# Second layer's normed rows and output rows turned between weight chunks, squares by block, linear attention's half products in turn, narrow products loaded wide

## The reference, cut

```
for l in range(2):                     # first block
    h  = rms(x,  norm_w[l]) * (1 + scale)   + shift      # 256 latent rows
    hc = rms(xc, norm_w[l]) * (1 + scale_c) + shift_c    # 256 context rows
    ... = project_stream(h, w_in[l], ...)                # 2048 -> 4160 + 2048 (z) columns
    x = x + gate * ((concat(o_a, o_b, o_c) * silu(z)) @ w_out[l])
    # xc likewise in layer 0 only

def gla_chunked(q, k, v, log_a):       # second block, 4 heads, chunks of 64 rows
    def step(state, xs):
        q_c, k_c, v_c, dec = xs
        o = einsum('bhcd,bhde->bhce', q_c, state)
        state = state * dec + einsum('bhcd,bhce->bhde', k_c, v_c)
        return state, o
```

## Time and profile before

| | |
|---|---|
| median of 3 runs | 3891.92 us |
| the profiled execution | 3893.01 us |
| its span | 3891.2 us |
| mean granted clock of TensorE | 0.972 |
| PE, busy share | 94% |
| DVE, ACT | 52%, 43% |
| HBM read | 148 GB/s |

### The profile page before, as it was taken

One profiled execution on the slowest core, in us unless ns is written; L12 is line 12 of the kernel. 1 busy time (PEld: TensorE's weight loads), 2 busy tenths in 40 slices (PEclk: granted clock), 3 DMA queues, 4 the chain that ended last, 5 costly groups with the idle time before them and its releaser, 6 DMA issues.

```text
span 3891.2 us, 46277 instructions
## 1 busy us (share of the span) xinstructions
PE 3647.3 (94%) x18672; PEld 2943.5 (76%) x18672; DVE 2013.7 (52%) x3118; ACT 1670.0 (43%) x2696; POOL 68.0 (2%) x118
## 2 busy tenths in 40 slices
PE   7899999999898799999899999999999799999998
PEld 2677777887776677778677777766777599999776
DVE  1666654344567646642355544435455466666444
ACT  2323344434421423455544434444445555455433
POOL 1200000000020000000000000000000000000000
PEclk8999999999999999999999999999999999999999
DMA  9643322233364455223355566635555356666554
GB/s 363 187 146 114 98 60 55 58 103 100 108 191 150 134 173 179 87 64 108 93 180 160 160 178 178 179 103 159 179 173 178 103 163 186 188 185 188 180 184 162
DMA packets 351045, 577.49 MB, mean 148 GB/s; under 512 B 25316, under 2 KB 131060, under 8 KB 348912
## 3 DMA queue, kind: packets, MB, share of 16 engines
q1 hardware_dynamic: 344512, 549.47, 45.7%
q0 software_dynamic: 6320, 25.06, 2.3%
HBM read 570.26 MB, written 4.19 MB: 148 GB/s over the span
## 4 chain that ended last, share of the span: by engine, by line
PE 56%; DVE 4%; ACT 3%; DMA 2%; issue 1%; DVEq 0%; SPq 0%; ACTq 0%
PE ps L703 36%; PE ps L1576 13%; DVE w_lo L672 1%; PE ps L1272 1%; DMA raw_ring<-in_w_in_dram 1%; ACT w_hi L666 1%; PE ps L1076 1%; PE ps L1184 1%; PE ps L1453 1%; PE ps L1460 1%; PE ps L1157 1%; PE ps L1166 0%; PE ps L739 0%; DMA raw_ring<-in_w_proj_b_dram 0%; PE ps L1180 0%
## 5 line engine op out<-in xcount | busy, mean ns | idle before, releaser
L672 DVE TENSOR_TENSOR w_lo<-raw_ring,w_hi 128x1024 fp32r<-128x1024 f32 (+1 forms) x827 | 1007.0, 1223 | 1148.8 <-ACT w_hi L666 1147.6
L666 ACT CAST w_hi<-raw_ring 128x1024 fp32r<-128x1024 f32 (+1 forms) x827 | 861.0, 1047 | 1233.7 <-PE ps L703 518.0
L703 PE MATMUL ps<-w_hi,r_a 128*128 128x512 f32 x3552 | 1311.8, 408 | 54.2 <-DVE w_lo L672 22.3
L703 PE MATMUL ps<-w_lo,r_a 128*128 128x512 f32 (+1 forms) x2624 | 1040.8, 397 | 0.0
L703 PE MATMUL ps<-w_hi,r_b 128*128 128x512 f32 (+1 forms) x2272 | 864.7, 399 | 18.1 <-DVE w_lo L672 11.3
L703 PEld LDWEIGHTS ps<-w_hi,r_a 128*128 128x128 f32 x3552 | 676.7, 191 | 243.0 <-issue 64.2
L703 PEld LDWEIGHTS ps<-w_lo,r_a 128*128 128x128 f32 x2624 | 501.9, 191 | 114.1 <-issue 8.6
L703 PEld LDWEIGHTS ps<-w_hi,r_b 128*128 128x128 f32 x2272 | 436.7, 192 | 127.1 <-DVE w_lo L672 17.0
L1576 PE MATMUL ps<-r_a,w_hi 128*128 128x256 f32 x2816 | 498.7, 279 | 0.0
L1576 PEld LDWEIGHTS ps<-r_a,w_hi 128*128 128x128 f32 x2816 | 430.9, 188 | 0.0
L1576 PE MATMUL ps<-r_a,w_lo 128*128 128x256 f32 x1408 | 394.5, 280 | 0.0
(11 more groups left out here) (330 smaller groups left out, 2946.4 us busy)
## 6 DMA issues: line engine op xcount, KB each, us to landing
raw_ring<-in_w_in_dram SPq DMA_DIRECT2D x386, 512.0 KB, 3.7
raw_ring<-in_ffn_w_up_dram SPq DMA_DIRECT2D x176, 512.0 KB, 3.6
raw_ring<-in_w_ada_dram SPq DMA_DIRECT2D x128, 512.0 KB, 3.9
raw_ring<-in_w_out_dram SPq DMA_DIRECT2D x96, 512.0 KB, 3.7
raw_ring<-in_ffn_w_down_dram SPq DMA_DIRECT2D x88, 512.0 KB, 3.6
gla_arena<-in_w_ada_dram SPq DMA_DIRECT2D x64, 512.0 KB, 9.2
raw_ring<-in_w_proj_b_dram SPq DMA_DIRECT2D x32, 512.0 KB, 3.6
raw_ring<-in_w_proj_a_dram SPq DMA_DIRECT2D x16, 512.0 KB, 3.6
```

The lines of the kernel that those rows point to most:

```text
L666: nc.scalar.copy(WH[:, ph.s_slot(i, j), 0:n], RAW[:, ph.raw_slot(i, j), 0:n]).then_inc(hi_ready, 1)
L672: nc.vector.tensor_tensor(WL[:, ph.raw_slot(i, j), 0:n], RAW[:, ph.raw_slot(i, j), 0:n], WH[:, ph.s_slot(i, j), 0:n].bitcast(F32), ALU.sub ...
L703: mm = nc.tensor.matmul(PS[:, t, a:z], X(x, k, t), W[w][:, kk * cols + a:kk * cols + z], start=(k == 0 and q == 0), stop=(c == len(js) - 1 ...
```

## The change

It has five parts.

1. The normed rows of layer 1: ACT squares blocks 0 to 2 while `wout0` runs, and block 3 behind it, tile after tile; the first two `w_hi` and a table load are put ahead. The scaling is done in two halves of the columns, with semaphores of their own. PE turns four blocks, and the other twelve two at a time behind chunks 0 to 5 of `win1` block 0; ACT and DVE follow in that order.
2. The output rows of layer 1: four blocks are turned ahead of `wout1`, the other twelve four at a time behind its chunks 0 to 2, the gates behind chunks 3 and 4.
3. Linear attention: `delta(0)` and `delta(1)` alternate d by d, in banks 2, 3 and 4, 5; `inter(2)` and `inter(3)` alternate; the state has three buffers; `delta(2)` and `inter(1)` stand together behind chunk 5.
4. `pe_narrow` loads 128 columns instead of 64 for k up to 14 of `kpe`, and writes 128 partitions, of which 64 are used.
5. In `wout1` ACT's squares stand behind `split(q+2)` instead of ahead.

```
     # pe_narrow
-                    mm = nc.tensor.matmul(PS[0:cols, 0, 0:act_k.shape[1]],
-                                          W[w][:, k * cols:(k + 1) * cols], act_k,
-                                          start=(k == 0 and q == 0), stop=(k == KT - 1 and q == 2))
+                    m = P if cols == ROPE and k < KT - 1 else cols
+                    mm = nc.tensor.matmul(PS[0:m, 0, 0:act_k.shape[1]],
+                                          W[w][:, k * cols:k * cols + m], act_k,
...
     # PE, entry of layer 1
-                    pe.wait_ge(act_x, l + 1)
-                    pe.wait_ge(dve_x, l + 1)
+                    pe.wait_ge(act_half, 1)
+                    pe.wait_ge(dve_half, 1)
                     pe.wait_ge(tr_free, TRN[f"h{l}"][0])
-                    for k in range(KT):
+                    for k in range(4):
                         group(TRN[f"h{l}"][0] + k, tr_tiles(lambda t: X4[:, t, k * P:k * P + P], 4))
...
                         pe_with_sum(pe, "win", l, b, c, WT[l][b])
+                        if l and b == 0 and c < 6:
+                            if c == 2:
+                                pe.wait_ge(act_x, l + 1)
+                                pe.wait_ge(dve_x, l + 1)
+                            for k in (2 * c + 4, 2 * c + 5):
+                                group(TRN[f"h{l}"][0] + k, tr_tiles(lambda t: X4[:, t, k * P:k * P + P], 4))
...
     # PE, wout1
+                    for c in range(8):
+                        pe.wait_ge(tr_free, y0 + 2 * c + 2)
+                        pe_block_part(pe, ph, 0, S8, c, 2, NB, x1, range(2), AC["wout1"][0])
+                        if c < 3:
+                            if c == 2:
+                                pe.wait_ge(z_used, 16 * l + 4 * T)
+                            for k in range(4 * c + 4, 4 * c + 8):
+                                turn_y(k)
+                        if 3 <= c < 5:
+                            gate(2 * c - 6)
+                            gate(2 * c - 5)
...
     # PE, gla_body
-                delta(0)
+                for d in range(2):
+                    delta(0, d, 2 + d)
+                    mm = delta(1, d, 4 + d)
+                mm.then_inc(gl_dl, 1)
                 og_chunk(i, 4)
+                og_chunk(i, 5)
                 pe.wait_ge(gl_att, i + 1)
+                pe.wait_ge(gl_st, 3 * i + 2)
...
-                inter(1).then_inc(gl_o, 1)
-                delta(1)
-                og_chunk(i, 5)
-                pe.wait_ge(gl_st, 3 * i + 2)
-                inter(2)
-                delta(2)
+                for d in range(2):
+                    mm = delta(2, d, 2 + d)
+                mm.then_inc(gl_dl, 1)
+                for d in range(2):
+                    mm = inter(1, d)
+                mm.then_inc(gl_o, 1)
                 og_chunk(i, 6)
                 pe.wait_ge(gl_st, 3 * i + 3)
-                inter(3).then_inc(gl_o, 1)
+                for d in range(2):
+                    inter(2, d)
+                    mm = inter(3, d)
+                mm.then_inc(gl_o, 1)
                 og_chunk(i, 7)
...
     # ACT, entry of layer 1
-                    act.wait_ge(acc_free, AC["win1"][0][0])
-                squares([(JUNK, X4[:, t], SS[:, t:t + 1]) for t in range(4)], ss_ready)
+                    act_hi(act, PH["win1"], 0, 0)
+                    act_hi(act, PH["win1"], 0, 1)
+                    warm_root()
+                    for t in range(4):
+                        act.wait_ge(acc_free, AC["wout0"][3][0] + t + 1)
+                        part_squares(X4[:, t, 3 * NB:D], t, 3, JUNKV, ss_ready if t == 3 else None)
...
+                    for h in range(2):
+                        for t in range(2):
+                            x = X4[:, t, D // 2 * h:D // 2 * h + D // 2]
+                            ins = nc.scalar.activation(x, x, ACT.Copy, scale=RINV[:, t:t + 1])
+                        ins.then_inc(act_x if h else act_half, 1)
...
     # ACT, wout0
+                    if l == 0 and b and c == 3:
+                        act.wait_ge(acc_free, AC["wout0"][b - 1][0] + 4)
+                        for t in range(4):
+                            part_squares(X4[:, t, NB * b - NB:NB * b], t, b - 1, JUNKV)
...
     # DVE, entry of layer 1
+                if l:
+                    mean_parts("h1", 4, D)
+                    mean_rinv("h1", 4)
+                    for h in range(2):
+                        for t in (2, 3):
+                            x = X4[:, t, D // 2 * h:D // 2 * h + D // 2]
+                            ins = V.tensor_scalar(x, x, RINV[:, t:t + 1], None, ALU.mult)
+                        ins.then_inc(dve_x if h else dve_half, 1)
...
     # DVE, gla_body
+                dve.wait_ge(gl_dl, 2 * i + 1)
+                for d in range(2):
+                    ins = V.tensor_copy(STATE[0][:, d, :], PS[:, 2 + d, :])
+                ins.then_inc(gl_st, 1)
...
+                dve.wait_ge(gl_decs, i + 1)
+                state(1, 4)
+                rest(8 * i + 6)
+                rest(8 * i + 7)
+                dve.wait_ge(gl_dl, 2 * i + 2)
+                state(2, 2)
+                rest(8 * i + 8)
                 rest(8 * i + 9)
```

143 lines of the change are left out of this document (84 added, 59 removed).

## The result

The changed kernel took 3873.74 us (median of 7 runs, 3867.56 to 3882.4) beside 3894.74 for the kernel before (7 runs, 3890.62 to 3896.69): a ratio of 0.9948, 95% interval 0.9936 to 0.996, 0.52% or 21.0 us faster. The forecast was 3874, 3864 to 3885. The runs of the changed kernel spread over 15 us with the mean clock that PE was granted: 3867.56 to 3870.68 at 0.975, 3882.4 at 0.971.

The account below looks back on a forecast made before the run. PE, busy 94% of the span, was taken as the bound. Terms -11.4 (entry), -2.2 (output rows), -5.1 (linear attention) and +0.2 (wide loads) sum to -18.5 us, giving 3874 us, range 3864 to 3885.

Parts of the forecast that it names:

- Entry: Start of the second layer: shorter PE hole and transposes between win1's chunks gain 11.4 us, bounds 8.5 and 14.4.
- chunk 0 and its transposes wholly at half clock: Entry of the second layer: win1's first chunk follows a long hole, so it and its transposes cost 3.0 us more.
- Output rows: Second layer's wout1: earlier transposes gain 2.5 us, 0.3 lost to the reload; gain 2.2, range 0 to 3.
- the turning alone: wout1: chunk 0 starts 5.2 us earlier, twelve groups of transposes come back between chunks; net gain 2.5 us.
- Linear attention: Four heads: overlapped pairs save 7.6 us after a new wait, less 2.5 for clock; gain 5.1, bounds -14 and +15.
- row halves run side by side: Delta(0) and delta(1) in each head use different operand partitions and overlap, saving 1.9 us, bounds 0 and 1.9.
- the new stand: Each linear-attention head: PE waits 1.9 us for DVE's second state update, behind chunk 7's w_lo, where before it had none.
- half-clock stretches behind the stands: Linear attention: one or two of the four new PE waits lower the clock, costing 2.5 us.
- The main rival: Linear attention gives nothing: row halves run serially or each wait drops the clock; 3878.5 to 3892.5 us, 24%.
- the two small ones: Linear attention's new wait does not come, 3863.5 us (10%); second-layer entry's early start fails through a late save, 3881 (3%).
- Wide narrow loads: kpe products loading 128 columns instead of 64: 0.2 us slower, bounds 0 and 1.0 slower.
- The clock rival: Clock stays at 0.50 in block 0 of win1 and wout1, and all four head waits drop it; 3919 us, 5%.

Follow-up runs that it names:

- f_reload: The changed kernel, but POOL issues the four constant loads behind the rows' reload only once block 0 of wout1 is added to the rows; 3865.5 us, ratio 0.9925 to before.
- gla_apart: The changed kernel, but PE takes og chunk 7 between inter(2) and inter(3) of each head; 3893.07 us, ratio 0.9992 to before.
- best: The changed kernel with constant loads behind wout1's block 0, state update ahead of chunk 7's w_lo, own semaphore for first two saves, narrow kpe loads; 3859.84 us.
- f_state: The changed kernel, with DVE's w_lo of a head's chunk 7 behind the second state update instead of ahead; 3865.99 us, ratio 0.9921 to before.
- p_gla: The kernel before with only the linear attention part of the change; 3885.81 us, ratio 0.9978 to before.
- gla_serial: The changed kernel, with both products of delta(0) ahead of both of delta(1), and inter(2), inter(3) likewise; 3874.0 us, ratio 0.994 to before.
- narrow_off: The changed kernel with the kpe products loading 64 columns again, as before; 3879.04 us in a single run.
- turns_first: The changed kernel, but in the second layer all 16 groups of four transposes stand ahead of win1's first chunk; 3879.72 us, ratio 0.9954 to before.

## Why the prediction was right, and where it was not

**The total**, 21.0 us against 18.5, holds three misses, not all of one sign. By the places of the trace the terms were -13.4, +0.9, -8.4 and +0.3, together -20.6: entry and linear attention gave 2.0 and 3.3 us more than forecast, the output rows 3.1 less. That so little is left of them is luck, and so is the last digit of the forecast: the kernel before has a median of 3894.74 in its seven runs, and the forecast had set out from 3891.92 in three and 3893.0 in the profile.

**Entry: -13.4 for -11.4.** The steps held: a hole of 7.27 us against the forecast's 7.2, ended by ACT's half scaling behind the save; chunk 0 18.2 us earlier against 18.1; the groups between the chunks at 0.88 us. Mis-sized was the clock: the forecast had chunk 0 and its transposes wholly at half clock (3.0), but the clock came back in the middle of the chunk and cost 1.6 (29.44 us for the block, less 8 x 2.8 and 5.4). This is as much the execution as the forecast: by the same sum it cost 0.4 in `f_reload` and 3.2 in `gla_apart`, so the forecast's 3.0 is the upper end of what the traces show, and the entry is worth 11.9 to 14.7 us by them. The other 0.6 is in the block before: I ended it with its last product, and the next block started 0.6 later, which the new one does not.

**Output rows: +0.9 for -2.2.** The step that failed is "the reload of the rows and what is queued behind it on POOL starts some 6 us later and now meets chunks without gates between; I take 0.3 for it, bounds 0 and 2". It measured 2.9 to 4.0: `f_reload` and `best`, without it, are 2.9 and 4.0 us shorter here than the changed kernel, and `best` is 3.1 shorter than before, more than the 2.5 that I had reckoned for the turning alone. I had the right transfers and the right cause, but priced them without following the ring. A weight chunk issued behind 3.7 MB lands after 10 us, in both kernels; the ring holds five chunks; four chunks of 3.4 to 3.7 us cover that, as before, and two of 4.2 and 4.5 followed by chunks of 2.8 do not. And the stand it makes is not only PE's wait: DVE's evacuation, which PE needs, stands behind the `w_lo` of the late chunk. The upper bound of 2 should have been the whole difference between the two landing times, 10.0 and 3.5.

**Linear attention: -8.4 for -5.1.** The mechanism was right in both halves: row halves run side by side like column halves (the 1.9 us chosen between 0 and 1.9), and the new stand came to 1.78 us against 1.9, by the chain that I named; `f_state` removed it by moving one instruction. Mis-sized was the clock again: I took 2.5 us for half-clock stretches behind the stands, and none came, behind any of the 32 stands in the eight traces that have them. The other 0.8 is four heads at 2.1 instead of 1.9. The 1.82 us in front of the transposes before did bring such a stretch, and the 1.78 us ahead of dense products here did not. The length of a stand doesn't decide it: a wait of 1.7 to 2.3 us for DVE's `w_lo`, some 50 us behind the last head in all thirteen traces, was followed by half clock in nine (after 1.79 us in the changed kernel, at 2698.90) and by full clock in four (after 2.18 us in `p_gla`). What does was not tried. The wording "in turn they can overlap" was too strict: `gla_serial` shows that they overlap in any order as neighbours. The main rival, that this part gives nothing (24%), is refuted, and so are the two small ones: the stand came, and so did the early start.

**Wide narrow loads: +0.3 for +0.2**, by `narrow_off`; the term has the right sign and no gain stands against it.

**The clock rival** (5%) rested on the rule that transposes do not count for the clock. The Trainium skill (TensorE: Matmul & The Clock Gate, Part 4: PE-mode transpose) says so; in `turns_first` the clock went from 0.51 to 0.82 to 1.00 with transposes alone on PE. The trace disagrees with the rule, if these transposes are of the page's mode, which no view shows, and from 1317 us on the block ran at full clock.

## What to carry to other kernels

When work between weight chunks is removed or moved, the pace of the chunks changes, and with it how long the ring covers a late landing: follow each chunk from its issue to its landing past every transfer that starts nearby, those queued behind the one in view above all, and delay the ones that nobody needs yet. When a product is moved a chunk later, look on the other engines for what now stands ahead of its successor in their queues; here one line's move gave 7 us. And products that use only half of the array's rows or columns should stand next to those of the other half; their order among themselves did not matter.
